# Block 2 of a two-block mixer with its positions grouped modulo sixteen, and score matmuls fed from queries in contiguous blocks

## The reference: what is computed

```python
DILATED_PATTERNS = ((128, 1), (512, 4), (2048, 16))

def dilated_window_attn(q, k, v, window, dilation):
    # positions are regrouped by residue mod d, giving a plain window of window//d
    B, S, H, hd = q.shape
    L = S // dilation
    def to_res(t):
        return t.reshape(B, L, dilation, H, hd).transpose(0, 2, 1, 3, 4).reshape(B * dilation, L, H, hd)
    o, lse = banded_window_attn(to_res(q), to_res(k), to_res(v), window // dilation)
    ...

def second_block(x, norm_pre_g, w_in, conv_w, w_out, norm_post_g):
    h = rmsnorm(x, norm_pre_g)
    z = jnp.einsum('bsd,de->bse', h, w_in)
    q, k, v, g_attn, c_h, c_b, c_c, g_conv = jnp.split(z, cuts, axis=-1)
    q, k = rope(q, pos), rope(k, pos)
    for window, dilation in DILATED_PATTERNS:
        o_i, lse_i = dilated_window_attn(q, k, v, window, dilation)
    mix_w = jax.nn.softmax(jnp.stack(lses, axis=0), axis=0)
    o = jnp.sum(mix_w[..., None] * jnp.stack(outs, axis=0), axis=0)
    attn_out = o * jax.nn.silu(g_attn)
    conv_out = c_b * causal_depthwise_conv(c_c * c_h, conv_w) * jax.nn.silu(g_conv)
    y = jnp.einsum('bse,ed->bsd', jnp.concatenate([attn_out, conv_out], axis=-1), w_out)
    return x + rmsnorm(y, norm_post_g)
```

## Time and profile before

| | us |
|---|---|
| median of 3 runs (lowest to highest) | 2617.68 (2610.38 to 2623.08) |
| the profiled execution's own time | 2614.59 |
| its span, first to last instruction | 2612.8 |
| TensorE busy | 2393.4 (92%) |
| VectorE, ScalarE, GpSimd busy | 1414.2, 840.9, 681.2 |
| the projection of block 1 ends, block 2 begins | about 1068 to 1084 |
| rope and gate stages | about 1240 to 1831 |
| attention stage, first score matmul to first matmul of the projection | 1845.16 to 2391.91 |

### The profile page before, as it was taken

The page is one execution under the profiler, slowest core; times in us unless marked ns, Lnnn a source line. Parts: engine busy times, 40 slices in busy tenths (PEclk is TensorE's granted clock), DMA queues, the critical chain, the costliest instruction groups (busy, mean ns, idle before and its releaser), DMA issues.

```text
span 2612.8 us, 47838 instructions
## 1 busy us (share of the span) xinstructions
PE 2393.4 (92%) x18958; PEld 2144.8 (82%) x18958; DVE 1414.2 (54%) x3441; ACT 840.9 (32%) x1938; POOL 681.2 (26%) x652
## 2 busy tenths in 40 slices
PE   6999899796999799699999999999699899897898
PEld 5977899796677688599888888889698899896777
DVE  6414768854798454663465533131476676675322
ACT  4411111111567110253122211011475676565111
POOL 0002011153231689200110111110105344443222
PEclk9999899898799899899999999999899999998999
DMA  4341320135640233332455531111858866964442
GB/s 148 113 104 55 102 72 23 58 99 154 178 114 22 101 121 109 121 126 94 143 188 164 175 98 65 49 61 49 200 150 194 204 171 165 203 196 153 147 140 103
DMA packets 283761, 322.19 MB, mean 123 GB/s; under 512 B 38049, under 2 KB 221217, under 8 KB 280081
## 3 DMA queue, kind: packets, MB, share of 16 engines
q1 hardware_dynamic: 281712, 313.09, 41.4%
q0 software_dynamic: 1680, 5.51, 0.7%
q10 hardware_dynamic: 144, 0.52, 0.0%
HBM read 196.91 MB, written 109.56 MB: 117 GB/s over the span
## 4 chain that ended last, share of the span: by engine, by line
PE 67%; DVE 10%; DMA 8%; issue 7%; POOL 3%; SPq 3%; ACT 2%; DVEq 0%; POOLq 0%; ACTq 0%
PE bank L163 50%; DMA cm<-scr_part 4%; PE bank L1779 3%; PE bank L1808 3%; DVE acc L642 3%; PE bank L1780 3%; PE bank L1790 3%; SPq L1899 1%; PE bank L1031 1%; PE bank L352 1%; DMA yn<-scr_y 1%; ACT bf L375 1%; POOL yo L2057 1%; PE bank L1023 1%; DVE bst L312 1%
## 5 line engine op out<-in xcount | busy, mean ns | idle before, releaser
L163 PE MATMUL bank<-w1h,xh 128*128 128x256 f32 (+1 forms) x896 | 260.7, 291 | 15.1 <-DVE s1st L632 15.1
L163 PE MATMUL bank<-w1l,xh 128*128 128x256 f32 (+1 forms) x896 | 256.5, 286 | 0.0
L163 PE MATMUL bank<-w1h,xl 128*128 128x256 f32 (+1 forms) x896 | 256.3, 286 | 0.0
L163 PE MATMUL bank<-xh,w2h 128*128 128x512 f32 x640 | 249.0, 389 | 0.0
L163 PE MATMUL bank<-xl,w2h 128*128 128x512 f32 x640 | 249.0, 389 | 0.0
L163 PE MATMUL bank<-xh,w2l 128*128 128x512 f32 x640 | 249.0, 389 | 0.0
L163 PE MATMUL bank<-w2h,xh 128*128 128x256 f32 x768 | 220.4, 287 | 10.9 <-issue 6.5
L1845 DVE CUSTOM_DVE_ANT_0 s2m<-bank,mask 128x256 f32<-128x256 f32 (+1 forms) x576 | 186.6, 362 | 72.0 <-PE bank L1780 68.4
L163 PE MATMUL bank<-w2h,xl 128*128 128x256 f32 x768 | 219.7, 286 | 0.0
L163 PE MATMUL bank<-w2l,xh 128*128 128x256 f32 x768 | 219.6, 286 | 0.0
L642 DVE SCALAR_TENSOR_TENSOR acc<-ain,cw,acc 128x512 f32<-128x512 f32 x240 | 200.3, 836 | 8.9 <-ACT acc L599 1.8
(11 more groups left out here) (256 smaller groups left out, 6215.6 us busy)
## 6 DMA issues: line engine op xcount, KB each, us to landing
v<-scr_v SPq DMA_DIRECT2D x12, 1552.0 KB, 9.7
scr_part<-ob SPq DMA_DIRECT2D x48, 264.0 KB, 3.2
cm<-scr_part SPq DMA_DIRECT2D x48, 264.0 KB, 4.6
w2r<-in_w_in SPq DMA_DIRECT2D x12, 1024.0 KB, 6.2
qr<-qf SPq DMA_DIRECT2D x192, 64.0 KB, 2.0
scr_v<-bvo SPq DMA_DIRECT2D x24, 388.0 KB, 2.5
v<-scr_v SPq DMA_DIRECT2D x24, 388.0 KB, 5.8
ax<-in_x SPq DMA_DIRECT2D x16, 512.0 KB, 6.3
```

The lines of the kernel that those rows point to most:

```text
L163: ins = nc.tensor.matmul(dst, x, y, start=k == 0 and m == 0, stop=k == n - 1 and m == 2)
```

## The change

The positions of block 2 are stored in another order: position 16 l + r stands at place 128 r + l, so all positions of one residue modulo sixteen are neighbours. x1 is stored by `project_stage` in that order (each tile of 128 positions goes to 16 groups of 8 rows), and so block 2's norm can begin only when all of x1 is stored (it waited for its own four tiles before). Queries, keys, values, gates and convolution come out in that order; the rotation tables are read at a step of 16, the convolution's neighbours stand 128 places apart, and the result is stored at a step of 16 rows.

In the attention stage d = 16 now comes first in head pairs 0 to 4 and last in pair 5. A block of 128 queries of d = 16 is contiguous. For d = 4 and d = 1 a block of queries consists of 4 runs of 32 places or 16 runs of 8 places; GpSimd copies the queries of four units into a contiguous buffer `qd` (two copies of 128 x 512, six to eight units ahead), and TensorE loads its weights from there. Keys are read in place, in runs of 128, 32 or 8. TensorE does the score matmuls of two units at a time, 8 matmuls in a row. The values for d = 1 are stored a second time in its own row order (`v21`), and the masks of d = 4 and d = 1 are loaded in row order by 4 and 16 loads and reordered by VectorE. `kept` now holds d = 16, and the stored parts are those of d = 4 and 1, each in its own row order, so step A takes 8 loads of 66 KB in place of 2 of 264 KB. Step A comes 2, 10, 18 and 26 units after the last gather and B eleven units after A. The buffer `sm` goes; masked scores are written to `p2r`, of which there are six.

```diff
 def norm_stage ... sp_fetch(g):
-                elif x_ready is not None:
-                    sp.wait_ge(*x_ready[t])
+                elif t == 0:
+                    for token in x_ready:
+                        sp.wait_ge(*token)
...
+                            for m, dst in enumerate(outs[n](i)):
+                                nc.sync.dma_start(dst, src if m == 0 else src[:, m - 1, :]).then_inc(*v_out[(e - 1) % 2].up(16))
...
 def project_stage
+            return x1.rearrange("(r t l) c -> t l r c", r=16, t=NT)[n]
-        return [(x_out[t], x_out[t].base + 16) for t in range(4)]
+        return [s.now() for s in (*x_out, x_last)]
...
 def rope_stage
+                cos, sin = (b[:].rearrange("p (l r) -> p r l", r=16)[:, 4 * x["g"]:4 * x["g"] + 4, :] for b in (cosT, sinT))
...
 def dilated_stage
+        ORDER = PATTERNS[::-1]
+        pairs = [(j, d) for j in range(6) for d in (ORDER if j < 5 else ORDER[::-1])]
-            mixing.append([t, [None] * delay + ["A"] + [None] * (3 if j < 5 else 0) + list("BCDEFG")])
+            mixing.append([t, [None] * delay + ["A"] + [None] * (10 if j < 5 else 0) + list("BCDEFG")])
-                        mix(j, quarter, quarter == 3, 9 * quarter, "pool", work)
+                        mix(j, quarter, quarter == 3, 2 + 8 * quarter, "pool", work)
+            if s % 2 == 0 and s - s % 4 + 8 in fours:
+                work.append(("reorder", s - s % 4 + 8, s % 4 // 2))
...
 pe_unit, scores
-                pe.wait_ge(*before)
-                q0, k0 = x["r"] + d * 128 * x["b"], x["r"] + d * 128 * (x["b"] - x["nk"] + 1)
-                qc, kc = slice(q0, q0 + d * 127 + 1, d), slice(k0, k0 + d * (w - 1) + 1, d)
-                for hh in range(2):
-                    dst = bank[:, 256 * hh:256 * hh + w]
-                    nc.tensor.matmul(dst, buf[hh][:, qc], buf[2 + hh][:, kc], start=True, stop=False)
-                    ins = nc.tensor.matmul(dst, buf[hh][:, qc], buf[4 + hh][:, kc], start=False, stop=True)
-                ins.then_inc(*p_s.up())
+                if d < 16:
+                    pe.wait_ge(*g_q.at(2 * (x["of4"] + 1)))
+                for x in two:
+                    for second in (False, True):
+                        for hh in range(2):
+                            g, k0 = x["g"], x["g"] - x["nk"] + 1
+                            dst = x["s"][hh].rearrange("p (t r l) -> p t r l", t=x["nk"], l=8 * d)
+                            q = buf[hh][:, 128 * g:128 * g + 128] if d == 16 else qd[x["of4"] % 3][hh][:, g % 4, :]
+                            keys = buf[(4 if second else 2) + hh]
+                            ins = nc.tensor.matmul(dst, q, blocks(keys[:], d)[:, k0:g + 1], start=not second, stop=second)
+                ins.then_inc(*p_s.up(2))
...
 pool_unit
+            if item[0] == "reorder":
+                if n >= 3:
+                    pool.wait_ge(*p_s.at(fours[n - 3] + 4))
+                nc.gpsimd.tensor_copy(qd[n % 3][hh][:].rearrange("p t (r l) -> p t r l", l=8 * d), blocks(qk[j % 2][hh][:], d)[:, g:g + 4]).then_inc(*g_q.up())
...
 sp_unit, mix A
-                for n in range(2):
-                    nc.sync.dma_start(cm[slot][:, :, n, :], part[n][j][rows, :].rearrange("(t p) c -> p t c", p=128)).then_inc(*cm_in[slot].up(16))
+                for n, d in enumerate((4, 1)):
+                    for i in range(4):
+                        t = 4 * q + i
+                        src = part[d][j].rearrange("(r b s l) c -> r s b l c", r=d, b=NT // d, s=STRIPES[d])[t % d, t // d]
+                        nc.sync.dma_start(cm[slot][:, i, n, :], src).then_inc(*cm_in[slot].up(16))
...
-        nc.sync.dma_start(mask2[:], A["c_mask2"]).then_inc(*m_in.up(16))
+        nc.sync.dma_start(mask[16][:], A["c_mask2"][:, 128:256]).then_inc(*m_in.up(16))
+        for d in (4, 1):
+            for r in range(STRIPES[d]):
+                nc.sync.dma_start(pr[d // 4][8 * d * r:8 * d * r + 8 * d, 0, :], A["c_mask2"].rearrange("(l r) k -> r l k", r=STRIPES[d])[r]).then_inc(*m_in.up(16))
```

More of the change, by code:

```diff
@@ L1566, in dilated_stage @@
         a_ph, a_ex, a_row, a_mix = sem("a_ph"), sem("a_ex"), sem("a_row"), sem("a_mix")
-        d_mx, d_pl, d_row, d_min, d_rec, d_mix = (sem("d_" + n) for n in ("mx", "pl", "row", "min", "rec", "mix"))
-        g_zero, g_mix = sem("g_zero"), sem("g_mix")
-        pairs = [(j, d) for j in range(6) for d in (PATTERNS if j < 5 else PATTERNS[::-1])]
+        d_mx, d_pl, d_row, d_min, d_rec, d_mix, d_mask = (sem("d_" + n) for n in ("mx", "pl", "row", "min", "rec", "mix", "mask"))
+        g_zero, g_q, g_mix = sem("g_zero"), sem("g_q"), sem("g_mix")
+        ORDER = PATTERNS[::-1]
+        pairs = [(j, d) for j in range(6) for d in (ORDER if j < 5 else ORDER[::-1])]
         N = 16 * len(pairs)
@@ L1578, in dilated_stage @@
                 units.append(dict(n=n, j=j, d=d, g=g, r=r, b=b, nk=nk, w=128 * nk, v0=r * nb + b - nk + 1))
+        fours = [u for u in range(0, N, 4) if units[u]["d"] < 16]
+        for n, u in enumerate(fours):
+            for x in units[u:u + 4]:
+                x["of4"] = n
         work, later, mixing, n_mix = [], [], [], 0
@@ L1665, in dilated_stage @@
                 x = units[item[1]]
-                x["s"] = sbk.take(d_mx.at(2 * item[1] + 2))
-                if x["d"] > 1:
-                    if x["g"] % 4 == 0:
-                        n_ob += 1
+                u = item[1]
+                x["s"] = [banks[u // 2 % 2 * 2 + hh][:, 256 * (u % 2):256 * (u % 2) + x["w"]] for hh in range(2)]
+                x["s_before"] = s_before if u < 4 else [d_mx.at(2 * (u - 4) + 4)]
+                if x["d"] < 16:
+                    n_ob += x["g"] % 4 == 0
                     x["ob"] = n_ob - 1
@@ L1763, in pe_unit @@
         def pe_unit(item):
-            if item[0] == "scores":
-                u, x = item[1], units[item[1]]
-                j, d, w, buf = x["j"], x["d"], x["w"], qk[x["j"] % 2]
-                bank, before = x["s"]
+            if item[0] == "scores" and item[1] % 2 == 0:
+                two = units[item[1]:item[1] + 2]
+                x = two[1]
+                j, d, buf = x["j"], x["d"], qk[x["j"] % 2]
                 if j == 0:
-                    for c in range(x["g"] // 4 + 1 if d == 1 else 4):
+                    for c in range(x["g"] // 4 + 1 if d == 16 else 4):
                         pe.wait_ge(*q0_in[c].at(160))
@@ L1877, in pool_unit @@
         def pool_unit(item):
-            if item[0] == "mix":
+            if item[0] == "reorder":
+                _, u, hh = item
+                pool.wait_ge(*g_zero.at(4))
+                x = units[u]
+                j, d, g, n = x["j"], x["d"], x["g"], x["of4"]
+                if n >= 3:
+                    pool.wait_ge(*p_s.at(fours[n - 3] + 4))
+                for token in [q.at(160) for q in q0_in] if j == 0 else [qk_in[j % 2].at(160 * ((j + 1) // 2))]:
+                    pool.wait_ge(*token)
+                nc.gpsimd.tensor_copy(qd[n % 3][hh][:].rearrange("p t (r l) -> p t r l", l=8 * d), blocks(qk[j % 2][hh][:], d)[:, g:g + 4]).then_inc(*g_q.up())
+            elif item[0] == "mix":
                 m = mixes[item[1]]
@@ L2173, in two_block_program @@
         with stack() as s2:
-            norm_stage("b", s2, x1, g2T, None, REST, x1_first, True, xh, xl, False, wts, [values(c) for c in range(3)], (2, 4), True)
+            norm_stage("b", s2, x1, g2T, None, REST, x1_done, True, xh, xl, False, wts, [values(c) for c in range(3)], (2, 4), True)
             wait_all(hand_over())
```

134 lines of the change are left out of this document (75 added, 59 removed).

## The result

The changed kernel takes **2683.4 us** (median of 4 runs, 2673.7 to 2686.3) against 2619.8 of before in the same comparison (4 runs, 2610.4 to 2623.1): a ratio of 1.0242, 95% interval 1.0203 to 1.0281. It is slower by 64 us; forecast were 2541 us and a gain. The profiled execution took 2680.8 us, its span is 2679.0.

The account below looks back on a forecast made before the run. TensorE, 92% busy, was taken as the bound, with DMA close behind. Pairs 1 to 4 -83, pair 0 -3, pair 5 +5, between the blocks +6: -75 from 2614.6, stated as 2541 us, range 2500 to 2596 for 8 in 10.

Parts of the forecast that it names:

- Pairs 1 to 4: Attention stage, head pairs 1 to 4: from 89.5 to 68.8 us each, -83 us in all, close to the DMA work.
- Saving on TensorE, 16.2 a pair: Attention scores: contiguous query weights make score matmuls cheaper at all three dilations, 16.2 us a head pair.
- The wait for `cm` goes, -8.5: Attention mixes: B eleven units after A removes 6.7 us of TensorE idle time and 1.8 of low clock a pair.
- +4 of new stall, bounds 0 and 10: Attention mixes: two of four may stall VectorE by up to 3 us each; 4 us a pair taken.
- Slower: `cm` comes late at every mix: Rival, attention: step A waits for G and the queue, B holds VectorE, twenty mixes at 8 us; 2645 us, chance 0.07.
- DMA is the bound: Rival, attention: 66 to 70 us of DMA work hold a pair at 75 us; 2566 us, chance 0.15.
- Copies on GpSimd in time: Attention: query copies at 0.6 us cost 0; the rival, late copies at 1.2 us, 2565 us, chance 0.11.
- Half-rate keys: Rival, attention scores: keys in short runs are read at half rate; 2617 us, no change, chance 0.08.
- Head pair 0: First attention pair: -16.2 for scores, +10 for mask loads ahead of queries, +3 for late loads; -3 us.
- Pair 5: Last attention pair: first two phases save 5, the last phase with three mixes costs 10; +5 us.
- Between the blocks: Start of block 2's norm: its first load waits for the last store of x1; +6 us (4 to 9).
- Norm stage: Block 2's norm stage: two extra stores of values a tile, beside 5.5 us of matmuls; 0.

Follow-up runs that it names:

- stores_act: The changed kernel with the 48 stores of parts issued from ScalarE's queue instead of SyncE's: 2652.0 us, ratio 1.0136.
- old_gap: The changed kernel with steps A and B of a mix at their earlier places, B four units after A: 2673.9 us, ratio 1.0224.
- best: The changed kernel with act_spread, kept_by_quarter, the masks of d = 4 and 1 loaded behind pair 0's queries, and a third `vo` buffer: 2587.7 us, ratio 0.9888.
- act_spread: stores_act with the next pair's ten query and key loads issued one every fourth unit from unit 0: 2611.5 us, ratio 0.9959.
- before_no_qk: The kernel before the change, without the query and key loads of head pairs 2 to 5: 2582.2 us, ratio 0.9856.
- kept_by_quarter: The changed kernel with a row block of kept waiting only for its own quarter's mix: 2666.2 us, ratio 1.0177.
- no_qk: The changed kernel without the query and key loads of head pairs 2 to 5: 2617.2 us, ratio 0.999.
- best_no_qk: best without the query and key loads of head pairs 2 to 5: 2568.8 us, ratio 0.9802.
- before_three: The kernel before the change with stores of parts from ScalarE's queue, spread query and key loads, and kept rows waited for by quarter: 2584.2 us, ratio 0.9853.
- two_loads: The changed kernel with step A in two loads of 264 KB instead of eight of 66 KB: 2670.3 us, ratio 1.021.

## Why the prediction was wrong

**The step that failed** is "Pairs 1 to 4: 89.5 - 16.2 - 6.7 - 1.8 + 4 = 68.8 us ... This lies at the 66 to 70 us of DMA work". They took 95.6 each; those 107 us, and 34 more at the smaller places below, are nearly all of the miss of 142. (The sum itself had a slip: 2540 and the 3 us added to it make 2543, not 2541.) Its parts:

- *Saving on TensorE, 16.2 a pair.* Right in mechanism and nearly in size: 14.2 measured. Two units of d = 16 take 2.02 us (2.08 forecast), of d = 4 with 256 keys 2.9 (before 4.1 to 4.4), of d = 1 3.27 where I had 3.12, for the keys in runs of 8.
- *The wait for `cm` goes, -8.5.* It shrank from 51.1 to 21.2 us over the four pairs, but VectorE now stood for the stores. Where the stores were out of the way (stores_act), or the gap was the old one (old_gap), the wait for `cm` was 68.0 and 98.3. The same backlog held it either way.
- *+4 of new stall, bounds 0 and 10.* This is the term that was wrong, by a factor of about six: 22 to 26 us idle a pair and a clock of 0.86. I had let the DMA floor work as a mean: 66 to 70 us of work fit into 69. The work was right: share times time is 68 us a pair before (0.76 x 89.5), 69 after (0.72 x 95.6), 68 in best (0.90 x 76.0). But on one queue in program order, ten query and key loads, values and four steps A stood between units 6 and 34. The term's own working had the issue of a step A at 3.6 us; with the queue free it was 4.7 to 5.6, in the changed kernel 8.2 to 13.5. My reading is that the burst had been covered by the slow matmuls that the change took away: a burst that is spread costs the changed kernel far less (act_spread). But the change also put the long units of d = 1 behind the burst and the short ones of d = 16 before it, and no run kept the old order of the dilations, so the two are not told apart. Before already paid 8.4 us a pair for it (before_no_qk), which the earlier trace rows had told me as the wait that I took for mended.
- *Overlooked: what the gap of ten units does to the kept rows.* I had followed step A past its G, and not the last G to the next user of kept. 15.9 us (kept_by_quarter).

By the experiments: these loads account for 68.3 us of pairs 1 to 4 (no_qk), kept rows for 15.9 (kept_by_quarter). With both gone, and the stores on ScalarE's queue, a pair takes 70.2 us against 68.8 forecast, so the sum of the terms was sound where nothing else bound. But with every load in place the shortest pairs of any run took 76.0 (best), with 68 us of DMA work in them; no run came to 68.8.

**The rivals.** "Slower: `cm` comes late at every mix", 2645 us at 0.07, was nearest: right in sign, and in the queue as the place. It named the wrong victim (a store, once a pair for 18 us, not `cm` at every mix) and was 38 us short. "DMA is the bound", 2566 us, had the right resource and priced only the mean. Copies on GpSimd in time: a copy took 0.617 us (0.6 forecast), and no wait of TensorE for them stands in the list. The Trainium skill (GPSIMD Engine Reference, section 3.1) has 769 ns for 512 elements; this trace is a fifth below it. Half-rate keys: refuted.

**Head pair 0**, -3: measured -0.5, that is +6.5 up to the first score matmul (+10 forecast) and -7.0 behind it (-13). The masks took 7.25 us of issue, and cost 7.0. Behind it TensorE still waits 9.7 us for queries, as it did for 10.3 before, and VectorE for a store, 5.7 us.

**Pair 5**, +5: measured +13.6. The last phase took 56.6 us against 54 forecast; VectorE waits 10.0 us for `cm` in it, as worked out there in kind. The first two phases took 1 us more instead of 5 less. TensorE, at the projection's first transpose, shows what the last phase ends on:

```profile
2450.30 1.51 PE L2043 MATMUL bank<-ident,yn 128*128 128x128 f32 x6 [20.49 <-DMA yn<-scr_y]
```

**Between the blocks**, +6: measured +10.9. Waiting for the last store cost 7, as forecast (4 to 9); that scattered packets "keep their 4 KB" and cost nothing was wrong by 4. Two rows of the changed kernel show it: ScalarE's queue and VectorE's first operation behind it, where the earlier trace rows stood at 1073.67.

```profile
1076.49 1.16 ACTq L1245 DMA_DIRECT2D scr_x<-xr  x1
```

```profile
1086.01 1.28 DVE L314 BATCH_NORM_STATS2 bst<-bx 128x6 f32<-128x512 f32 x2 [9.55 <-DMA bx<-scr_x]
```

**Norm stage**, 0: measured +8.8, of which 6.7 are the extra stores. They were "beside 5.5 us of matmuls", but a tile's buffer comes free only with the third store. A third buffer brought 7 of it back.

**Rope and gate**, 0: right (measured -1.5). The rotation's multiplies grew from 1111 and 777 ns to the ones below, in the changed kernel's costliest groups by form, and stayed under TensorE's cover.

```profile
L1395 DVE TENSOR_TENSOR qf<-qf,cosT 128x512 f32<-128x512 f32 x48 | 70.9, 1477 | 46.5 <-DMA qr<-qf 46.5
L1396 DVE TENSOR_TENSOR qr<-qr,sinT 128x512 f32<-128x512 f32 x48 | 54.5, 1136 | 0.0
```

**The projection**, 0: measured +7.8. From its first transpose to the end, before and changed (columns as above):

```profile
2391.91:2612.80 220.89, 194.78 (x864) 159.28 (x864) 65.34 (x172) 38.97 (x100) 47.79 (x32) 0.94 0.42 139
2450.30:2679.00 228.70, 197.18 (x864) 161.54 (x864) 67.94 (x177) 38.73 (x101) 47.54 (x32) 0.92 0.43 140
```

TensorE stands idle for 5.4 us more, and is busy for 2.4 us more at the lower clock. The idle time is in its waits for `yn` (the rows that it projects, loaded from memory), 17.6 us against 12.1 behind the first one. Why they land later no run took apart. Nor was it tried where best's remaining 10.5 us in pair 5 come from; its trace puts them at the end, where TensorE stands 20.3 us for `yn` and before_three 6.8. That the last sum of x1 falls anywhere from 1069.7 to 1082.1 us in the profiled executions of these kernels is left unexplained.

## What to carry to other kernels

A mean DMA share times the length of a stretch gives the work, and is a floor only if the queue is fed evenly. Before counting a saving on the engine that bounds, lay out what the queue must carry in each part of the loop, and ask which compute covered the burst. A wait for a transfer that stands in the list now (52 us for `cm`) is the sign that the cover is already thin, and moving its consumer back changes its name, not its length. The cheapest test is to leave one bulk load out: here that separated the matmul saving from the queue. And try the cures in the old kernel as well: here it was as fast with them (2584.2 us) as the changed kernel with its own (2587.7).

## What the runs showed of the hardware

- The issue of a transfer took longer when much stood on its queue: one 512 KB load took 9.31 us to issue, against 0.60, and eight loads of 66 KB took 8.2 to 13.5 us against 4.7 to 5.6 without the query and key loads. Everything behind them on that queue waited, stores for which a buffer was wanted among them. With fewer loads ahead (two_loads) one later load took 16.17 us instead.
- The issue of the same 512 KB store took 1.16 us with scattered rows where it took 0.34 with whole ones.
- Keys of a matmul in runs of 8 float32, 128 places apart, cost 0.016 us on 0.130 for 256 columns; runs of 32 cost nothing that shows.
- A two-input operation of VectorE on 128x512 whose one operand is read at a step of 16 float32 took 1477 and 1136 ns against 1111 and 777.
- Stalls cost twice: as pairs 1 to 4 lost their idle time, the granted clock rose from 0.86 (changed) over 0.91 (act_spread) and 0.96 (best) to 1.00 (best_no_qk), and TensorE's busy time for the same 4375 operations from 284.5 over 284.3 and 275.4 to 266.2 us.
